# Order of the head pairs in the first mixer's attention: latent and context pairs mixed in place of one kind after the other

## What is computed

```python
def hybrid_na_sgu(h_ctx, h_lat, w_in, rpb, w_s, b_s, w_out, ctx_out):
    ...
    a_lat = neighbourhood_attention(heads(q), heads(k), heads(v), heads(kc), heads(vc), rpb)
    s_lat = spatial_gating(jax.nn.gelu(u), jax.nn.gelu(g), w_s, b_s)
    y_lat = jnp.concatenate([a_lat, s_lat], axis=-1) @ w_out
    ...
        a_ctx = context_attention(heads(qc), heads(kc), heads(vc))
        s_ctx = spatial_gating(jax.nn.gelu(uc), jax.nn.gelu(gc), w_s, b_s)
        y_ctx = jnp.concatenate([a_ctx, s_ctx], axis=-1) @ w_out
```

## Time and profile before

| | |
|---|---|
| median of 3 runs | 2115.49 us |
| the profiled execution's own time | 2116.14 us |
| its span on the core | 2114.3 us |
| PE busy with matmuls | 2043.5 us, 97% of the span |
| DVE busy | 1620.2 us, 77% |
| ACT busy | 1174.7 us, 56% |
| transfers from HBM | 180 GB/s over the span |
| the attention's turns on PE | 1116.3 to 1158.3 us of the span |

### The profile page before, as it was taken

How to read it: one execution, slowest core, us unless ns; L and a number is a source line. 1 busy time by engine, 2 the same in 40 slices (tenths; PEclk the granted TensorE clock), 3 DMA queues, 4 the chain that set the end, 5 groups by cost and what they waited for, 6 DMA issues and landing times.

```text
span 2114.3 us, 36831 instructions
## 1 busy us (share of the span) xinstructions
PE 2043.5 (97%) x13880; PEld 1850.6 (88%) x13880; DVE 1620.2 (77%) x2681; ACT 1174.7 (56%) x2109; POOL 125.0 (6%) x213
## 2 busy tenths in 40 slices
PE   6999999999999999998999999999998999999998
PEld 6988989999988989998876788888878888999997
DVE  7888879966688878978778879787889335657983
ACT  6757746645556746645637555353544236656862
POOL 0100000000000000004000100001000000000000
PEclk9999999999999999999999999999999999999999
DMA  9766547874666546875441434546553223244653
GB/s 369 271 208 200 176 154 249 269 239 161 223 231 207 176 164 225 290 254 194 159 150 40 160 120 150 180 149 223 185 189 130 96 94 100 90 146 135 197 181 110
DMA packets 106625, 383.03 MB, mean 181 GB/s; under 512 B 11505, under 2 KB 16129, under 8 KB 105185
## 3 DMA queue, kind: packets, MB, share of 16 engines
q1 hardware_dynamic: 77584, 280.21, 39.5%
q0 software_dynamic: 25792, 94.31, 13.4%
q10 hardware_dynamic: 3088, 6.29, 0.9%
HBM read 379.71 MB, written 1.05 MB: 180 GB/s over the span
## 4 chain that ended last, share of the span: by engine, by line
PE 88%; DVE 6%; ACT 3%; issue 1%; DMA 1%; SPq 0%; DVEq 0%; ACTq 0%
PE ps L1056 21%; PE ps L1059 21%; PE ps L1060 21%; PE ps L1075 3%; PE ps L1079 3%; PE ps L1080 3%; PE ps L1097 2%; PE ps L1100 2%; PE ps L1101 2%; DVE ring_l L2292 2%; PE ps L1609 1%; DVE ada_junk L2315 1%; ACT ring_r L1659 1%; DMA ring<-tape_in 1%; PE ps L1292 1%
## 5 line engine op out<-in xcount | busy, mean ns | idle before, releaser
L1056 PE MATMUL ps<-part,ring_l 128*128 128x256 f32 (+1 forms) x3400 | 1033.4, 304 | 15.2 <-DVE ring_l L2292 6.7
L1059 PE MATMUL ps<-part,ring_r 128*128 128x256 f32 (+1 forms) x3400 | 1025.8, 302 | 0.0
L1060 PE MATMUL ps<-part,ring_r 128*128 128x256 f32 (+1 forms) x3400 | 1022.8, 301 | 0.0
L1659 ACT ACTIVATE ring_r<-ring 128x1024 fp32r<-128x1024 f32 x514 | 533.9, 1056 | 390.1 <-DMA ring<-tape_in 292.1
L2292 DVE TENSOR_TENSOR ring_l<-ring,ring_r 128x1024 fp32r<-128x1024 f32 x514 | 623.9, 1227 | 158.2 <-ACT ring_r L1659 155.7
L1056 PEld LDWEIGHTS ps<-part,ring_l 128*128 128x128 f32 x3400 | 643.3, 189 | 50.3 <-issue 6.4
L1060 PEld LDWEIGHTS ps<-part,ring_r 128*128 128x128 f32 x3400 | 641.2, 189 | 26.0
L1059 PEld LDWEIGHTS ps<-part,ring_r 128*128 128x128 f32 x3400 | 641.5, 189 | 23.8
L2315 DVE SCALAR_TENSOR_TENSOR ada_junk<-work 128x1024 bf16<-128x1024 f32 x272 | 334.0, 1228 | 47.3 <-DMA work<-adas_in 35.2
L1097 PE MATMUL ps<-part,ring_l 128*128 128x256 f32 (+1 forms) x400 | 123.6, 309 | 16.5 <-DVE part L2292 11.0
L1100 PE MATMUL ps<-part,ring_r 128*128 128x256 f32 (+1 forms) x400 | 121.7, 304 | 0.0
(11 more groups left out here) (281 smaller groups left out, 2102.5 us busy)
## 6 DMA issues: line engine op xcount, KB each, us to landing
ring<-tape_in SPq DMA_DIRECT2D x514, 512.0 KB, 3.5
work<-adas_in POOLq DMA_DIRECT2D x176, 512.0 KB, 4.7
work<-ada_first_in SPq DMA_DIRECT2D x8, 1024.0 KB, 17.5
work<-bias_in ACTq DMA_DIRECT2D x1, 2048.0 KB, 8.2
x<-x_t_in SPq DMA_DIRECT2D x1, 1024.0 KB, 7.8
work<-cond_in POOLq DMA_DIRECT2D x1, 1024.0 KB, 8.8
x<-ctx_in ACTq DMA_DIRECT2D x1, 1024.0 KB, 7.6
x<-dist_in ACTq DMA_DIRECT2D x1, 1024.0 KB, 7.5
```

Of the source, the lines that this page charges most:

```text
L1056: mm = pe.matmul(dst, lhsT=wl, rhs=mr, start=(k == 0), stop=False)
L1059: pe.matmul(dst, lhsT=wr, rhs=mr, start=False, stop=False)
L1060: mm = pe.matmul(dst, lhsT=wr, rhs=ml, start=False, stop=(k == len(moving) - 1))
L1659: act.activation(ring_r[:, q % RING, :], ring[:, q % RING, :], ACT.Copy).then_inc(rounded, 1)
```

## The change

A table gives the order of the pairs, and everything that depended on `p < WT` asks the table instead. The turns are now latent 0, latent 1, context 0, latent 2, context 1, context 2, latent 3, context 3:

```diff
-def na_parts(p):
-
-
-    return range(4 * p, 4 * p + 4) if p < WT else range(2 * H + 2 * (p - WT), 2 * H + 2 * (p - WT) + 2)
+NA_TURNS = (0, 1, 4, 2, 5, 6, 3, 7)
+
+
+def na_own(turn):
+
+    return NA_TURNS[turn] < WT
+
+
+def na_tile(turn):
+
+    return NA_TURNS[turn] % WT
+
+
+def na_parts(turn):
+
+    first = sum(4 if na_own(n) else 2 for n in range(turn))
+    return range(first, first + (4 if na_own(turn) else 2))
...
             for part in na_parts(p):
-                BANK2[f"na_score{part}"] = 2 + (n if p < WT else 2 * (p % 2) + n)
+                BANK2[f"na_score{part}"] = 2 + part % 4
                 BANK2[f"na_keys{part}"] = (6 + part % 3) % BANKS
...
-                if p < WT:
+                if na_own(p):
                     dsts = {2 * q + a: open2(f"na_score{parts[2 * q + a]}") for q in rows for a in range(2)}
...
                 if p >= 1:
-                    t, cols = (p - 1) % WT, slice(0, T) if p - 1 < WT else slice(T, T2)
+                    t, cols = na_tile(p - 1), HALVES[0 if na_own(p - 1) else 1]
                     act.wait_ge(*done2(f"na_pv{p - 1}"))
...
-                if p >= WT:
+                if not na_own(p):
                     dve.wait_ge(*done2(f"na_score{parts[-1]}"))
...
-                        dve.wait_ge(*na_biased(part))
+                        dve.wait_ge(*na_biased(na_own_before(part)))
```

More of the change, by code:

```diff
@@ L350, in order_block1, with na_turn, na_half, na_own_before @@
     return o + [f"down{f}" for f in range(KD)]
-def na_parts(p):
-    return range(4 * p, 4 * p + 4) if p < WT else range(2 * H + 2 * (p - WT), 2 * H + 2 * (p - WT) + 2)
+NA_TURNS = (0, 1, 4, 2, 5, 6, 3, 7)
[6 more added lines that the diff above has]
+    return range(first, first + (4 if na_own(turn) else 2))
+def na_turn(part):
+    return next(turn for turn in range(H) if part in na_parts(turn))
+def na_half(part):
+    return (part - na_parts(na_turn(part))[0]) // 2
+def na_own_before(part):
+    return sum(na_own(na_turn(n)) for n in range(part))
 def order_block2():
@@ L371, in order_block2 @@
     for p in range(H):
-        early = 2 if p + 2 < WT else 0
+        early = 2 if p + 2 < H and na_own(p + 2) else 0
         o += [f"na_keys{part}" for part in na_parts(p)[:3]]
@@ L816, in na_exp_of @@
         def na_exp_of(part):
-            return part if part < 2 * H else 2 * H + 2 * (part - 2 * H) + 1
+            return sum(1 if na_own(na_turn(n)) else 2 for n in range(part + 1)) - 1
         HALVES = (slice(0, T), slice(T, T2))
@@ L877, in two_blocks @@
         for p in range(H):
-            for n, part in enumerate(na_parts(p)):
-                BANK2[f"na_score{part}"] = 2 + (n if p < WT else 2 * (p % 2) + n)
+            for part in na_parts(p):
+                BANK2[f"na_score{part}"] = 2 + part % 4
                 BANK2[f"na_keys{part}"] = (6 + part % 3) % BANKS
@@ L1475, in na_scores @@
                     dsts = [bank2(f"na_score{part}") for part in parts]
-                t = p % WT
+                t = na_tile(p)
                 sides = [(a, slice(64 * a, 64 * a + 64)) for a in range(2)]
@@ L1494, in na_by_keys @@
                     dst = open2(f"na_keys{part}")
-                    if p < WT:
-                        q, a = divmod(part % 4, 2)
+                    if na_own(p):
+                        q, a = na_half(part), part % 2
                         for k in range(4):
@@ L2157, in na_exps @@
                     n, src = 2 * p + a, bank2(f"na_score{part}")
-                    for q in ([part % 4 // 2] if p < WT else range(2)):
-                        cols = slice(0, T2) if p < WT else slice(q * T, (q + 1) * T)
-                        act.activation(na_probs[n % 4][q][:, 0:T2 if p < WT else T], src[:, cols], ACT.Exp, bias=na_max[:, n, q:q + 1],
+                    for q in ([na_half(part)] if na_own(p) else range(2)):
+                        cols = slice(0, T2) if na_own(p) else slice(q * T, (q + 1) * T)
+                        act.activation(na_probs[n % 4][q][:, 0:T2 if na_own(p) else T], src[:, cols], ACT.Exp, bias=na_max[:, n, q:q + 1],
                                        accum_out=na_sum[:, n, q:q + 1]).then_inc(na_exp.sem, 1)
@@ L2181, in _ @@
                         act.wait_ge(*done2(f"na_keys{part}"))
-                        if p < WT:
-                            q = part % 4 // 2
+                        if na_own(p):
+                            q = na_half(part)
                             act.activation(na_keys[a][:, :, q * P:(q + 1) * P], src.rearrange("p (k q) -> p k q", k=4), ACT.Copy)\
@@ L2962, in na_maxima @@
                         src = bank2(f"na_score{part}")
-                        dve.tensor_tensor(src[:, 0:T], src[:, 0:T], na_bias[:, q, 2 * p + part % 2, :], ALU.add).then_inc(na_biased.sem, 1)
+                        dve.tensor_tensor(src[:, 0:T], src[:, 0:T], na_bias[:, q, 2 * na_tile(p) + part % 2, :], ALU.add).then_inc(na_biased.sem, 1)
                     for part in both:
-                        dve.wait_ge(*na_biased(part))
+                        dve.wait_ge(*na_biased(na_own_before(part)))
                         dve.tensor_reduce(na_max[:, 2 * p + part % 2, q:q + 1], bank2(f"na_score{part}"), AX.X, ALU.max, negate=True)\
@@ L2973, in na_normalise @@
                 dve.wait_ge(*na_recips(p))
-                for q, a in ([(q, a) for q in range(2) for a in range(2)] if p < WT else [(q, a) for a in range(2) for q in range(2)]):
+                for q, a in ([(q, a) for q in range(2) for a in range(2)] if na_own(p) else [(q, a) for a in range(2) for q in range(2)]):
                     n = 2 * p + a
-                    part = na_probs[n % 4][q][:, 0:T2 if p < WT else T]
+                    part = na_probs[n % 4][q][:, 0:T2 if na_own(p) else T]
                     dve.tensor_scalar(part, part, na_recip[:, n, q:q + 1], None, ALU.mult).then_inc(na_probs_made.sem, 1)
```

12 lines of the change are left out of this document (5 added, 7 removed).

## The result

The changed kernel takes 2123.61 us, the median of 18 runs (2118.99 to 2129.94), against 2117.27 us for the kernel before in 18 runs (2111.09 to 2125.63). The ratio is 1.0029, with a 95% interval of 1.0019 to 1.0038: 6.1 us more, 4.0 to 8.0. When the changed kernel was timed again in another set of rounds, the ratio was 1.0032 (1.0018 to 1.0046). The forecast was 4.2 more and no change that counts. Taken as a difference, the stated range (2115.0 to 2123.5 beside 2115.49 before, so 0.5 less to 8.0 more) holds the result; 2123.61 itself lies 0.1 above its end, because the median of the kernel before came out 1.8 higher with more runs. Of the 0.3% that was set as the border, 1.0029 lies just under it and 1.0032 just over it, so it isn't shown on which side the change falls. The sign is as forecast, and the size forecast is two thirds of the one measured.

What follows compares the result with a forecast made beforehand. PE, busy 97% of the span, was taken as the bound. Longer waits of 2.8 plus one clock fall of 1.4 gave +4.2 us: 2120.3 profiled, 2119.7 us as median, 0.20% slower, counted as the same; range 2115.0 to 2123.5.

Steps and rivals of the forecast that it cites:

- What bounds the kernel: Whole kernel: PE busy 97% of the span; this attention stage could give back some 3 us, 0.14%.
- The waits turn by turn: PE waits at turns 2, 3, 4 and 5 laid out as 1.3, 1.0, 0.05 and 3.4: +2.8 us over the old order.
- The fall of the clock: Behind turn 5's wait: one fall to half rate lasting 3.2 to 3.5 us, costing 1.4 us.
- The rest of the program: After the stage: its delay passes through whole to the end; 1.4 us either way.
- Rival 1: Stage: the longer waits without a fall of the clock, +2.8 us, 2118.3; chance 0.15.
- Rival 2: Clock falls at two places, turn 5 and one of turns 2 and 3: +5.6 us, 2121.1; chance 0.14.
- rival 3: Clock falls behind all three waits, turns 2, 3 and 5: 7.0 us, 2122.5, over 0.3% slower; chance 0.12.
- The rule on transposes: Turns 2, 3 and 5: if transposes don't count as busy for the clock, three falls, 7.0 instead of 4.2.
- Rival 4: Stage: the mix balances the engines, light turns giving DVE and ACT room; 2.66 us of waits go, 2112.8; chance 0.11.

Runs made afterwards that it cites:

- experiment 1: Changed kernel with 14 idle matmuls on PE in the place of its wait ahead of turn 5's transposes: stage 44.63 us, ratio 1.0012 to the kernel before.
- experiment 2: Changed kernel with DVE normalising turn 5 ahead of the maxima of turn 6: stage 46.62 us.
- experiment 3: Old order of pairs with four more DVE reductions, results unused, ahead of turn 5's normalisation: stage 46.68 us, ratio 1.0020.
- experiments 4 and 5: Changed kernel with table 0, 1, 2, 4, 3, 5, 6, 7: stage 41.43, ratio 1.0003; then also turns 2 and 3 normalised ahead of the maxima: 40.70, 1.0009.
- the run with 12 pairs: Old order with 24 idle matmuls (12 pairs) on PE after its wait ahead of turn 5's transposes: stage 48.90 us.

## Why the prediction was right, and where it was short

- **What bounds the kernel.** Right. The stage had under 3 us to give, and the best of the orders tried took 1.26 of it.
- **The waits turn by turn.** Right, and the best part of it: 1.3, 1.0, 0.05 and 3.4 were laid out, 1.12, 0.98, none and 3.42 came. The 2.8 us of longer waits are 2.7 by experiment 1. Experiments 2 and 3 show the mechanism: the wait sits where DVE's queue puts it, and it comes up in the old order too when that queue is as long.
- **The fall of the clock.** It comes where it was expected, at turn 5's wait, in four profiles of four, and nowhere else in the stage. The price was taken as 1.4 from the fall at 272.07. This is the term that was mis-sized: it is 1.3 to 1.5 in two profiles and 2.6 to 2.7 in the other two, because the fall can last 6.8 us. The forecast took one observed length of a fall, 3.2 to 3.5 us, for the only one. That a fall would come at all was a judgement between cases that had gone both ways (chance 0.48), and here it came in all four.
- **The rest of the program.** "I let the delay pass through whole" is neither shown nor refuted. Its own test was a difference of over 1 us between the delay of the stage and that of the end, and the timed rounds place the end only within 4.0 to 8.0. From the statistics to the first matmul of the next projection it is 13.7 us in all profiles but that of before, which had 14.4: the clock fell behind its wait of 1.94 ahead of 1203.34, which is at most 1.58 in the others. Behind that, the runs scatter by more than the change. The 6.1 us of the timed rounds, less the stage's mean of 4.7, leave 1.4, over the border of 1 us; the open stretch above would be 1.0 of it, but 4.7 lies inside the interval, so the timed rounds don't show that anything is left to explain.
- **Rival 1**, waits without a fall, is what experiment 1 makes of it, 44.63. **Rival 2**, a second fall, and **rival 3**, three falls, didn't happen: behind the waits of 1.12 and 0.98 the clock stayed at 1.00 in all four profiles. The timed 6.1 nevertheless came out nearer to rival 2's 5.6 than to the forecast's 4.2. The longer waits and one fall, of double length in two profiles of four, account for 4.7 of it; the timed number alone would have spoken for a second fall.
- **The rule on transposes.** The Trainium skill, "TensorE: Matmul & The Clock Gate", section "Part 4: PE-mode transpose", has transposes not count as busy for the clock. No run here shows the three falls that followed from it: the transposes behind the waits of 1.12 and 0.98 ran at full clock in all four profiles. The long falls of the changed kernel do end only when the transposes and the short matmuls behind them are over, as in 1151.24 above. But the profiles with a short fall had the same instructions, and in experiment 3 the long fall ended within the values, at 1152.43. So these runs don't decide on that rule.
- **Rival 4**, the balance. Its first half holds in part in experiments 4 and 5: there the wait of 1.37 ahead of turn 5 goes, since a heavy turn stands ahead of it on PE, but the light turn itself keeps waits around it. The table of the change puts two light turns right ahead of a heavy one, in the stretch where DVE also splits panels, and there it takes the room away. The output projection over turns 6 and 7 had no wait to cover.

## What to carry to other kernels

When work of two sizes goes through several engines, each with a written order, look at what the short piece on the bounding engine has to cover on the other one: a light turn on PE with a heavy successor's preparation ahead of its own in DVE's queue costs up to the difference of the two preparations (here 2.05 us more of waiting for 2.5 more of maxima). A stage laid out by hand from the rows, queue by queue, gave such waits to 0.2 us here; what it doesn't give is the clock, and at the wait of 3.42 us a fall of the clock cost 1.3 to 2.7 us beside the 2.7 of longer waits. Idle matmuls in the place of a wait that can't be removed took that part back.

## What the runs showed of the hardware

- In this stage the fall has two lengths, and which one comes goes with where it begins. It began 0.89, 0.79 and 1.63 us before PE went on in the first and third profiles of the changed kernel and in experiment 3, and lasted 6.8 us each time. It began 0.34 before and just as PE went on in the second and fourth, and 0.27 before in experiment 2; in the run with 12 pairs it began 0.55 after. Those four lasted 3.4. The wait and the instructions behind it were the same in the four changed profiles, so the kernel's instructions alone don't decide where the fall begins; what else does isn't shown.
- The same pair of waits, 0.30 and 1.38, left the clock whole in three profiles of the old order and was followed by a fall in the run with 12 pairs. The work right behind the second wait differs (transposes there, idle matmuls here), so this is no clean pair.
- At half clock the 64-row scores took 2.08 for 1.13 and the transposes 1.97 for 1.18, while the 128 x 256 matmuls of the earlier trace rows began every 0.214 us in the place of 0.12: a factor of 1.7 to 1.8 in each case.
- A clean pair stands near 750 us of the span, where the waits of 1.39 and 0.93 of the earlier trace rows come a second time. In the four profiles of the changed kernel the instructions and the two waits there are the same; the clock fell behind them in the second and fourth and stayed whole in the first and third. PE in the first and in the second:

```profile
753.78 0.39 PE L1080 MATMUL ps<-part,ring_l 128*128 128x256 f32 x1 [0.93 <-DVE part L2316]
...
754.24 0.28 PE L1080 MATMUL ps<-part,ring_l 128*128 128x256 f32 x1
```

```profile
754.74 0.44 PE L1080 MATMUL ps<-part,ring_l 128*128 128x256 f32 x1 [0.93 <-DVE part L2316]
...
755.41 0.42 PE L1080 MATMUL ps<-part,ring_l 128*128 128x256 f32 x1
```

So one profile without a fall behind such waits is no proof that they are harmless.
